# First stage of a hybrid encoder block: thirteen of 32 w_ada items multiplied by c on TensorE, small rows loaded through ScalarE's queue, gate transposes inside the second group

## The chip, the cores and the metric

One Trainium2 chip, of which the kernel uses one core. Time is the device time of one execution in microseconds (us). A core has TensorE (PE, matmuls; PEld its weight loads), VectorE (DVE), ScalarE (ACT), GpSimd (POOL) and SyncE (SP, which here only issues DMAs). Every engine runs its own instruction stream in order; semaphores tie them together.

## What is computed

One layer with a token mixer and an MLP, on x of 512 x 2048, each with RMSNorm and a shift, scale and gate that come from a conditioning vector c. The change lies in the part that these lines describe:

```python
c_act = jax.nn.silu(c)
mod = (c_act @ w_ada[i] + b_ada[i])[:, None, :]          # 2048 x 12288
shift_m, scale_m, gate_m, shift_f, scale_f, gate_f = jnp.split(mod, N_MOD, axis=-1)
h = rmsnorm(x, g_pre_mix[i]) * (1.0 + scale_m) + shift_m
proj = h @ w_in                                           # combined input projection
fq, fk, fv, ff, gq, gk, gv, ga, gr = jnp.split(proj, IN_OFFSETS, axis=-1)
log_f = jax.nn.log_sigmoid((ff + b_fgate).astype(jnp.float32))
```

What follows (forgetting attention on 8 heads, gated linear attention on 4, output projection, squared-ReLU MLP, residuals) is computed as before.

## The kernel before

All arithmetic is f32. A large product is made of three passes: each operand is split into a rounded part (`in_hi`, `w_hi`, written by ScalarE) and the rest (`in_lo`, `w_lo`, written by VectorE), and `split_mm` (L707 to L711) multiplies hi by hi, lo by hi and hi by lo.

The contraction over 2048 is cut into 16 steps k of 128 rows. The input projection runs in groups of six output tiles of 128 columns: group 0 (two heads of the forgetting attention), three more of these, then the GLA heads. One step of `group_steps` is 18 matmuls with 512 moving columns. Group 0 has besides three narrow ones each step (`wm_hi`, `wm_lo`: 16 gate-rank and 8 forget-gate columns), so 21. From group 1 on, small steps of the attention of the group before (`fox_slot`) are woven in between.

Group 0 can't use its input before scale and shift are there. Scale and shift for the mixer are 4096 columns of c_act @ w_ada. They are made in four blocks of 512 columns of either kind, and a block serves four steps k. A block is read as eight items (`load_am`, L537), each 256 rows of w_ada by 2 x 512 columns, 1 MB in two DMAs. Four buffers `am_item` hold items; item n is loaded when item n-4 has been used. `add_am` (L1662) on VectorE multiplies an item by its values of c, which are scalars of a partition, and adds to `am_acc`: two instructions of 128 x 1024. When all eight are in, TensorE sums over the 128 partitions with eight matmuls in which `am_acc` is stationary and one column of ones moves (`start_slot`, L901). `mod_columns_m` on VectorE adds the biases and gains (`mod_a`, `mod_b`), ScalarE writes `in_tmp` and `in_hi`, VectorE `in_lo`, and TensorE does the four steps. The items of the next block are multiplied meanwhile: VectorE's loop does two items after each step's `in_lo`.

Ahead of that, x comes in (`x_raw`), ScalarE squares it, POOL takes the root, VectorE scales it, TensorE transposes it in 64 pieces (L885) into six PSUM banks, and ScalarE and VectorE copy the banks to `xn_t`. Gains and biases arrive as rows (`rows_a`, `rows_b`, nine small DMAs by `as_rows`) on SP's queue behind the first four items, and are turned into columns (`cols_a`, `cols_b`); VectorE takes them between items 1 and 2 and scales x after item 3.

Between group 0 and group 1 the forget gate is made: VectorE and ScalarE compute log_sigmoid and a running sum (`f_z`), TensorE transposes it in four pieces (L937), ScalarE copies these to `cumq`, and TensorE waits for that copy before group 1. VectorE's order there is: gate operations, running sum, `w_lo` for group 1, eviction of its tiles of group 0.

Of the kernel before, what the change touches and what calls it, by code (L numbers as in the profile page):

```python
# [37 lines left out]
ALU = mybir.AluOpType  # L38
# [7 lines left out]
def build_block(nc, x, c, w_ada, b_ada, g_pre_mix, g_post_mix, w_in, b_fgate, w_gla_a2, b_gla_a2,  # L46
# [58 lines left out]
    with ExitStack() as ctx:  # L105
# [107 lines left out]
        decay = small("decay", [P, NCH])  # L213
        assert k_at[0] <= nc.sbuf_usable_end
# [64 lines left out]
        am_used = sem("am_used")  # L279
        am_sum = sem("am_sum")  # L280
# [91 lines left out]
        def arrived_mlp(b, mm):  # L372
            return RAW_MLP + 16 * (b * (MM_O // 2) + mm // 2 + 1)

# [80 lines left out]
        def _(sp):  # L455
# [79 lines left out]
            def as_rows(dst, src, done):  # L535
                sp.dma_start(dst, src.rearrange("o (k p) -> (o k) p", p=P)).then_inc(done, 16)

            def load_am(n):
                if n >= 4:
                    sp.wait_ge(am_used, n - 3)  # L540
# [9 lines left out]
            as_rows(rows_c[:, :], c[0:1, :], c_in)  # L550
# [6 lines left out]
            load_am(2)  # L557
            load_am(3)
            for n, src in enumerate((g_pre_mix[0:1, :], b_ada[0:1, SHIFT_M:SHIFT_M + D],
                                     b_ada[0:1, SCALE_M:SCALE_M + D], b_ada[0:1, SHIFT_F:SHIFT_F + D],  # L560
                                     b_ada[0:1, SCALE_F:SCALE_F + D], g_pre_mlp[0:1, :])):
                as_rows(rows_a[n * KT:(n + 1) * KT, :], src, rows_in)
            as_rows(rows_b[B_A2:B_GFOX, :], b_gla_a2, rows_in)
            sp.dma_start(rows_b[B_GFOX:B_GGLA, :], g_fox_out[0]).then_inc(rows_in, 16)
            sp.dma_start(rows_b[B_GGLA:20, :], g_gla_out[0].rearrange("h (k p) -> (h k) p", p=P)).then_inc(rows_in, 16)
            load_am(4)
            sp.wait_ge(wm_zero, 1)
            sp.dma_start(wm_raw[:, :, 0:RANK], w_in_t[:, :, GA_COL:GA_COL + RANK]).then_inc(wm_in, 16)
            sp.dma_start(wm_raw[:, :, 32:32 + FOX_HEADS], w_in_t[:, :, FF_COL:FF_COL + FOX_HEADS]).then_inc(wm_in, 16)
            sp.dma_start(b_fg[32:40, :], b_fgate.rearrange("o h -> h o")).then_inc(bfg_in, 16)  # L570
            load_am(5)
            load_fox(0, 0, wait=False)
            load_am(6)
            load_am(7)
# [131 lines left out]
        def _(pe):  # L706
# [6 lines left out]
            def group_steps(r, first, slot, misc_step=None):  # L713

                for k in range(KT):
# [10 lines left out]
                    for b in range(TILES):  # L726
# [10 lines left out]
                        if not first and b == 2:  # L737
                            slot(2 * k)
                    if not first:
                        slot(2 * k + 1)  # L740
# [13 lines left out]

            def fox_slot(s, f):

                if s == 0:
                    pe.wait_ge(ev_act, 3 * f + 3)
                    pe.wait_ge(ev_dve, 3 * f + 3)
                    for t in range(TB):  # L760
                        last = pe.transpose(BB[:, t * P:t * P + P], grp[:, VA, t * P:t * P + P], ident[:, :])
                    last.then_inc(fox_v_tr, 1)
# [5 lines left out]
                if s % 3 == 0 and s // 3 < 8:  # L768
                    j = s // 3
                    i = j % TB  # L770
                    if j:
                        pe.wait_ge(fox_max, 8 * f + j)
                    if j == 1:
                        pe.wait_ge(fox_v_tok, 2 * f + 2)
                    if j == 0:
                        pe.wait_ge(ada_col, 3 * f + Q_FOX)
                    q_tile, k_tile = (QA, KA) if j < TB else (QB, KB)
# [1377 lines left out]
```

## Time and profile before

| | us |
|---|---|
| median of three runs | 2357.48 (2356.92 to 2359.67) |
| profiled execution | 2364.44 |
| its span | 2362.4 |
| TensorE busy in the span | 2191.7 (93%) |
| VectorE busy | 1607.4 (68%) |
| ScalarE busy | 961.2 (41%) |
| group 0's matmuls, first to last | 62.67 to 177.33 |

All numbers of the sections below are from the profiled execution. Busy time of TensorE counts overlapping matmuls once. "Idle before" behind a row is the engine's idle time just before it, with what ended it. The granted clock (PEclk) is a share of 2.4 GHz: 0.50 is the lower level of 1.2 GHz. It is recorded where it changes; before the first change, at 54 us, the windows print 1.00.

### The profile page before, as it was taken

The page shows a single profiled execution, that of the slowest core. Times are in us where ns is not written, and L with a number is a line of the kernel's source. Part 1 is how long each engine was busy: PE and PEld are TensorE (multiplying, and loading weights), DVE is VectorE, ACT ScalarE, POOL GpSimd, SP SyncE. Part 2 cuts the span into 40 slices and gives each one's busy share as a digit, 9 for nine tenths or more (in the row PEclk, how much of TensorE's full clock was granted, in tenths as well). Part 3 has the DMA queues.
Part 4 walks back from the last instruction along what each step waited for, and adds up shares of the span by engine and source line. Part 5 has one row for each costly group of instructions (what it writes and reads, how often), then busy time and mean ns, then how long its engine had stood idle before and what let it go on. Part 6 is the DMA issues. An engine that isn't in the chain of part 4 may idle for free.

```text
span 2362.4 us, 26561 instructions
## 1 busy us (share of the span) xinstructions
PE 2191.7 (93%) x9759; PEld 1777.9 (75%) x9759; DVE 1607.4 (68%) x1418; ACT 961.2 (41%) x1445; POOL 489.3 (21%) x245
## 2 busy tenths in 40 slices
PE   2778999999999799989999999999989999999996
PEld 2566777777777577778888888888878888888875
DVE  5856666677787755466535436436469898998998
ACT  2225445444435423344434344344344444434443
POOL 0001221121111110110000000000026354544564
PEclk9889999999999999999999999999999999999998
DMA  8845545545555454256566666556346745766763
GB/s 310 302 166 148 160 135 149 154 132 156 156 159 162 128 200 130 71 183 209 214 209 196 219 200 211 212 191 227 134 143 214 246 161 187 243 214 208 273 207 150
DMA packets 335934, 441.09 MB, mean 187 GB/s; under 512 B 17036, under 2 KB 209744, under 8 KB 329816
## 3 DMA queue, kind: packets, MB, share of 16 engines
q1 hardware_dynamic: 335240, 435.51, 56.3%
q10 hardware_dynamic: 592, 4.21, 0.5%
q8 instruction: 66, 1.08, 0.2%
q14 instruction: 36, 0.29, 0.0%
HBM read 379.88 MB, written 59.79 MB: 186 GB/s over the span
## 4 chain that ended last, share of the span: by engine, by line
PE 56%; issue 31%; DVE 5%; POOL 5%; DVEq 1%; ACT 1%; POOLq 1%; DMA 0%; ACTq 0%
PE pair L709 18%; PE pair L711 18%; PE pair L710 18%; POOL ada L2030 3%; DVE acc L1506 1%; DVE v_op L1897 1%; POOL f_r L2063 1%; POOLq L2023 0%; POOL v_raw L2115 0%; PE pair L995 0%; POOL rstd L2024 0%; DVEq L1557 0%; ACT ada L1107 0%; DVE in_lo L1764 0%; DVE grp L1609 0%
## 5 line engine op out<-in xcount | busy, mean ns | idle before, releaser
L709 PE MATMUL pair<-in_hi,w_hi 128*128 128x512 f32 x1792 | 728.7, 407 | 10.9 <-DVE w_lo L1474 9.1
L711 PE MATMUL pair<-in_hi,w_lo 128*128 128x512 f32 x1792 | 705.7, 394 | 0.0
L710 PE MATMUL pair<-in_lo,w_hi 128*128 128x512 f32 x1792 | 705.5, 394 | 0.0
L1474 DVE TENSOR_TENSOR w_lo<-w_raw,w_hi 128x2048 fp32r<-128x2048 f32 (+1 forms) x142 | 301.2, 2121 | 379.1 <-ACT w_hi L1088 377.6
L1088 ACT ACTIVATE w_hi<-w_raw 128x2048 fp32r<-128x2048 f32 (+1 forms) x142 | 244.8, 1724 | 411.1 <-PE pair L711 337.4
L709 PEld LDWEIGHTS pair<-in_hi,w_hi 128*128 128x128 f32 x1792 | 341.4, 191 | 92.9 <-issue 20.9
L711 PEld LDWEIGHTS pair<-in_hi,w_lo 128*128 128x128 f32 x1792 | 340.5, 190 | 73.9
L710 PEld LDWEIGHTS pair<-in_lo,w_hi 128*128 128x128 f32 x1792 | 341.3, 190 | 70.1 <-issue 1.9
L709 PE MATMUL pair<-v_op,hid_r 128*128 128x512 f32 x896 | 349.9, 390 | 9.0 <-ACT v_op L1453 7.1
L711 PE MATMUL pair<-v_op,hid_r 128*128 128x512 f32 x896 | 349.3, 390 | 0.0
L710 PE MATMUL pair<-v_op,hid_r 128*128 128x512 f32 x896 | 349.3, 390 | 0.0
L1897 DVE TENSOR_TENSOR v_op<-v_raw,v_op 128x1024 fp32r<-128x1024 f32 x192 | 302.1, 1594 | 66.5 <-ACT v_op L1453 65.4
L1453 ACT ACTIVATE v_op<-v_raw 128x1024 fp32r<-128x1024 f32 x192 | 203.5, 1061 | 294.8 <-PE pair L711 280.2
L2030 POOL TENSOR_TENSOR ada<-ada,c_act 128x2048 f32<-128x2048 f32 x32 | 120.9, 3778 | 832.2 <-DMA ada<-in_w_ada 832.2
L1506 DVE TENSOR_REDUCE acc<-ada 128x128 f32<-128x2048 f32 x64 | 241.7, 3796 | 12.3 <-ACT ada L1107 12.0
L2106 POOL TENSOR_TENSOR v_sum<-v_raw,v_raw 128x512 f32<-128x512 f32 x64 | 157.1, 2482 | 350.5 <-DVE v_raw L1912 350.5
L709 PEld LDWEIGHTS pair<-v_op,hid_r 128*128 128x128 f32 x896 | 168.7, 188 | 45.8 <-ACT v_op L1453 7.5
L711 PEld LDWEIGHTS pair<-v_op,hid_r 128*128 128x128 f32 x896 | 168.6, 188 | 35.2
L710 PEld LDWEIGHTS pair<-v_op,hid_r 128*128 128x128 f32 x896 | 168.7, 188 | 35.1
L1107 ACT ACTIVATE ada<-ada,c_act 128x128 f32<-128x128 f32 x512 | 155.4, 388 | 6.4 <-DMA ada<-in_w_ada 6.4
L2115 POOL TENSOR_TENSOR v_raw<-v_raw,v_sum 128x512 f32<-128x512 f32 x64 | 143.3, 2269 | 18.5 <-DVE v_op L1897 18.4
L1928 DVE TENSOR_TENSOR y_t<-pair,y_t 128x1024 f32<-128x1024 f32 x104 | 125.0, 1215 | 0.9 <-PE pair L711 0.8
(194 smaller groups left out, 1908.1 us busy)
## 6 DMA issues: line engine op xcount, KB each, us to landing
ada<-in_w_ada SPq DMA_DIRECT2D x64, 1024.0 KB, 7.0
w_raw<-in_w_mlp_in SPq DMA_DIRECT2D x64, 1024.0 KB, 5.3
v_raw<-in_w_mlp_out SPq DMA_DIRECT2D x128, 512.0 KB, 4.9
hid_r<-hid_scratch SPq DMA_DIRECT2D x112, 512.0 KB, 6.3
hid_scratch<-hid_r SPq DMA_DIRECT2D x28, 1792.0 KB, 7.2
am_item<-in_w_ada SPq DMA_DIRECT2D x64, 512.0 KB, 5.2
w_raw<-in_w_in SPq DMA_DIRECT2D x128, 256.0 KB, 3.7
w_raw<-in_w_in SPq DMA_DIRECT2D x128, 128.0 KB, 3.5
```

The source lines that it names most:

```text
L709: pe.matmul(dst, a[0], b[0], start=start, stop=False, skip_group_check=onto)
L710: pe.matmul(dst, a[0], b[1], start=False, stop=False, skip_group_check=onto)
L711: return pe.matmul(dst, a[1], b[0], start=False, stop=stop, skip_group_check=onto)
L1088: act.activation(w_hi[n][:, view], w_raw[n][:, view], ACT.Copy).then_inc(hi_done, 1)
L1107: last = act.activation(ada0[0][:, k, :], ada0[0][:, k, :], ACT.Copy, scale=c_act[:, k:k + 1])
L1453: act.activation(v_op[i % 4][:, 0, :], raw_of(u, p)[:, h, :], ACT.Copy).then_inc(v_hi, 1)
L1474: dve.tensor_tensor(w_lo[n][:, view], w_raw[n][:, view], w_hi[n][:, view].bitcast(F32), ALU.subtract)\
L1506: dve.tensor_reduce(acc[:, u * P:(u + 1) * P], ada0[u][:, :, :].rearrange("p k n -> p n k"), AX_X, ALU.add).then_inc(ada_acc[u], 1)
L1897: dve.tensor_tensor(v_op[i % 4][:, 1, :], raw_of(u, p)[:, h, :], v_op[i % 4][:, 0, :].bitcast(F32), ALU.subtract).then_inc(v_lo, 1)
L2030: pool.tensor_tensor(unit[:, :, :], unit[:, :, :], c_act[:, :].rearrange("p (k o) -> p k o", o=1).to_broadcast([P, KT, P]), ALU.mult)\
L2106: last = pool.tensor_tensor(v_sum[:, h, cols], v_raw[q[B22]][:, h, cols], v_raw[q[B11]][:, h, cols], ALU.add)
L2115: last = pool.tensor_tensor(b21, b21, v_sum[:, h, cols], ALU.subtract)
```

## The change

- *Products of c on TensorE.* `AM_PE` names the items that TensorE takes: 1, 3, 5 and 7 of block 0, and 1, 3 and 5 of the other three blocks. `am_columns` does an item as 16 matmuls: a 128 x 128 piece of the item is stationary and one column of `c_act` moves; two row pieces are accumulated into one PSUM column. An item has eight columns of its own in bank 6. `mod_columns_m` adds the parts with one `tensor_reduce`, then goes on as before. VectorE keeps the other 19 items. An item that TensorE takes frees its buffer by `am_mul` instead of `am_used`.
- *Places.* Item 1 stands before the transposes of x, items 3, 5 and 7 behind them. Items 1, 3 and 5 of the next block stand before steps 1, 2 and 3 of the block at work. VectorE does items 0 | 2 | 4, 6 around the scaling of x and the eviction, and in a block items 0 | 2, 4 | 6, 7 after steps 1, 2 and 3.
- *Small rows.* The nine row loads go out first on ScalarE's queue; the two loads of narrow w_in columns and `b_fg` follow there behind the squares of x. SP's queue keeps c, x, the items and w_in.
- *Gate transposes.* The four transposes of `f_z` move from the gap between the groups into group 1, behind its third tile; the first logit moves behind its fifth tile, where TensorE waits for `cumq`. Group 1 is written out; the loop starts at group 2.

```diff
+        AM_PE = [(1, 3, 5, 7)] + [(1, 3, 5)] * 3
...
             def load_am(n):
                 if n >= 4:
-                    sp.wait_ge(am_used, n - 3)
+                    if on_pe(n - 4):
+                        sp.wait_ge(am_mul, items_before(n - 3, True))
+                    else:
+                        sp.wait_ge(am_used, items_before(n - 3, False))
...
+            def am_columns(n):
+                col = AM_COL + 8 * (1 + AM_PE[n // 8].index(n % 8))
+                pe.wait_ge(am_in[n % 4], 32 * (n // 4 + 1))
+                for part in range(2):
+                    for j in range(4):
+                        for kk in range(2):
+                            k = 2 * (n % 8) + kk
+                            last = pe.matmul(BA[:, col + 4 * part + j:col + 4 * part + j + 1],
+                                             am_item[n % 4][:, kk, part, j * P:j * P + P], c_act[:, k:k + 1],
+                                             start=kk == 0, stop=kk == 1)
+                last.then_inc(am_mul, 1)
+
+            am_columns(1)
             for k in range(KT):
                 if k == 0:
                     pe.wait_ge(xn_ready, TB)
+                    pe.wait_ge(cols_ready, 1)
...
+            for n in AM_PE[0][1:]:
+                am_columns(n)
...
             def start_slot(s):
...
+                if s % 8 and s // 8 < 3:
+                    if s % 8 == 2:
+                        pe.wait_ge(am_col, s // 8 + 1)
+                    am_columns(8 * (s // 8 + 1) + AM_PE[s // 8 + 1][s % 8 // 2 - 1])
                 if s % 8 == 0:
                     block = s // 8
-                    pe.wait_ge(am_used, 8 * (block + 1))
+                    pe.wait_ge(am_used, items_before(8 * (block + 1), False))
...
-            pe.wait_ge(cum_ready, 1)
-            for t in range(TB):
-                last = pe.transpose(BA[:, t * FOX_HEADS:(t + 1) * FOX_HEADS], f_z[32:40, t * P:t * P + P],
-                                    ident[32:40, 32:40])
-            last.then_inc(cumq_tr, 1)
-            pe.wait_ge(cumq_ready, 1)
-            with pe.Fori(1, FOX_GROUPS) as r:
+            group_steps(1, False, first_fox_slot, early=first_logit)
+            with pe.Fori(2, FOX_GROUPS) as r:
...
+            for n, src in enumerate((g_pre_mix[0:1, :], b_ada[0:1, SHIFT_M:SHIFT_M + D],
...
+                as_rows(rows_a[n * KT:(n + 1) * KT, :], src)
...
+            act.wait_ge(wm_zero, 1)
+            act.dma_start(wm_raw[:, :, 0:RANK], w_in_t[:, :, GA_COL:GA_COL + RANK]).then_inc(wm_in, 16)
+            act.dma_start(wm_raw[:, :, 32:32 + FOX_HEADS], w_in_t[:, :, FF_COL:FF_COL + FOX_HEADS]).then_inc(wm_in, 16)
...
-            for n in range(2):
-                add_am(n)
+            add_am(0)
...
-            for n in range(2, 4):
-                add_am(n)
...
-            for n in range(4, 6):
-                add_am(n)
+            add_am(2)
...
+                dve.wait_ge(am_mul, items_before(8 * (block + 1), True))
+                parts = BA[:, AM_COL:AM_COL + 8 * (1 + len(AM_PE[block]))].rearrange("p (s c) -> p c s", c=8)
+                dve.tensor_reduce(am_tot[:, :], parts, AX_X, ALU.add)
...
-            for n in range(6, 8):
+            for n in (4, 6):
                 add_am(n)
...
-                    for n in range(8 + 2 * k, 10 + 2 * k):
-                        add_am(n)
+                    for i in ((), (0,), (2, 4), (6, 7))[k % 4]:
+                        add_am(8 * (k // 4 + 1) + i)
```

TensorE from its first instruction to the first matmuls of group 0, before (a row's names are output, moving operand, stationary operand; `pair` is PSUM):

```order
L875 MATMUL pair<-ident,rows_c 128x16
L877 MATMUL pair<-ident,rows_a 128x96
L878 MATMUL pair<-ident,rows_b 128x20
L885 MATMUL pair<-ident,x_raw 128x128 x64
L901 MATMUL pair<-ones,am_acc_86 128x1 x8
L709 MATMUL pair<-in_hi,wm_hi 40x512
```

and the same place of the changed kernel, where L894 is a product of c and L927 the sum over the partitions:

```order
L881 MATMUL pair<-ident,rows_c 128x16
L883 MATMUL pair<-ident,rows_a 128x96
L884 MATMUL pair<-ident,rows_b 128x20
L894 MATMUL pair<-c_act,am_item_83 128x1 x16
L907 MATMUL pair<-ident,x_raw 128x128 x64
L894 MATMUL pair<-c_act,am_item_85 128x1 x16
L894 MATMUL pair<-c_act,am_item_83 128x1 x16
L894 MATMUL pair<-c_act,am_item_85 128x1 x16
L927 MATMUL pair<-ones,am_acc_86 128x1 x8
L708 MATMUL pair<-in_hi,wm_hi 40x512
```

Item 1 now stands ahead of the transposes, and items 3, 5 and 7 stand between them and the sum.

VectorE from the first column sums on, through one block of four steps, before:

```order
L1720 TENSOR_TENSOR mod_a<-mod_a,cols_a 128x4
L1726 TENSOR_TENSOR wm_lo<-wm_raw,wm_hi 128x640
L1707 TENSOR_TENSOR w_lo_78<-w_raw_74,w_hi_76 128x1536
L1702 TENSOR_TENSOR in_lo<-in_tmp,in_hi 128x512
L1676 TENSOR_SCALAR am_acc_87<-am_item_82,c_act 128x1024
L1674 SCALAR_TENSOR_TENSOR am_acc_87<-am_item_82,c_act,am_acc_87 128x1024
L1674 SCALAR_TENSOR_TENSOR am_acc_87<-am_item_83,c_act,am_acc_87 128x1024 x2
L1702 TENSOR_TENSOR in_lo<-in_tmp,in_hi 128x512
L1707 TENSOR_TENSOR w_lo_79<-w_raw_75,w_hi_77 128x1536
L1674 SCALAR_TENSOR_TENSOR am_acc_87<-am_item_84,c_act,am_acc_87 128x1024 x2
L1674 SCALAR_TENSOR_TENSOR am_acc_87<-am_item_85,c_act,am_acc_87 128x1024 x2
```

and changed:

```order
L1771 TENSOR_TENSOR mod_a<-mod_a,cols_a 128x4
L1777 TENSOR_TENSOR wm_lo<-wm_raw,wm_hi 128x640
L1754 TENSOR_TENSOR w_lo_78<-w_raw_74,w_hi_76 128x1536
L1749 TENSOR_TENSOR in_lo<-in_tmp,in_hi 128x512 x2
L1754 TENSOR_TENSOR w_lo_79<-w_raw_75,w_hi_77 128x1536
L1727 TENSOR_SCALAR am_acc_87<-am_item_82,c_act 128x1024
L1725 SCALAR_TENSOR_TENSOR am_acc_87<-am_item_82,c_act,am_acc_87 128x1024
L1749 TENSOR_TENSOR in_lo<-in_tmp,in_hi 128x512
L1725 SCALAR_TENSOR_TENSOR am_acc_87<-am_item_84,c_act,am_acc_87 128x1024 x2
L1725 SCALAR_TENSOR_TENSOR am_acc_87<-am_item_82,c_act,am_acc_87 128x1024 x2
```

The first two `in_lo` now come in a row, and one item instead of two pairs stands ahead of the third.

## Rows read from the trace of the kernel before

**Rows 1.** The page's slices of about 59 us, busy tenths of TensorE and VectorE.

```profile
PE   2778999999999799989999999999989999999996
DVE  5856666677787755466535436436469898998998
```

**Rows 2.** Windows, all engines: second and last block of group 0; columns in the heading.

```profile
core 0: us, PE busy (x) PEld busy (x) DVE busy (x) ACT busy (x) POOL busy (x), PEclk, DMA share, GB/s
93.67:124.74 31.07, 23.97 (x100) 18.07 (x101) 26.17 (x26) 8.32 (x11) 0.00 (x0) 0.88 0.92 322
156.16:177.33 21.17, 21.17 (x84) 15.98 (x84) 5.85 (x7) 6.32 (x8) 0.00 (x0) 0.91 0.13 37
```

**Rows 3.** Timeline of VectorE, third block; start us, duration, operation, [idle before].

```profile
129.27 0.69 DVE L1702 TENSOR_TENSOR in_lo<-in_tmp,in_hi 128x512 fp32r<-128x512 f32 x1
129.87 1.75 DVE L1474 TENSOR_TENSOR w_lo<-w_raw,w_hi 128x1536 fp32r<-128x1536 f32 x1
131.71 5.38 DVE L1674 SCALAR_TENSOR_TENSOR am_acc<-am_item,c_act,am_acc 128x1024 f32<-128x1024 f32 x4
...
152.95 0.16 DVE L1717 TENSOR_TENSOR mod_b<-pair,cols_a 128x4 f32<-128x4 f32 x1 [2.04 <-PE pair L901]
```

**Rows 4.** Timeline of TensorE, from the second block's end to the fourth's start.

```profile
117.34 0.39 PE L711 MATMUL pair<-in_hi,w_lo 128*128 128x512 f32 x1
119.91 1.95 PE L901 MATMUL pair<-ones,am_acc 128*128 128x1 f32 x16 [2.17 <-DVE am_acc L1674]
...
124.74 0.62 PE L709 MATMUL pair<-in_hi,wm_hi 128*40 128x512 f32 x1 [2.89 <-DVE in_lo L1702]
...
131.69 0.40 PE L709 MATMUL pair<-in_hi,wm_hi 128*40 128x512 f32 x1
...
156.16 0.62 PE L709 MATMUL pair<-in_hi,wm_hi 128*40 128x512 f32 x1 [3.25 <-DVE in_lo L1702]
```

**Rows 5.** Timeline, the first column sums.

```profile
55.40 3.54 PE L901 MATMUL pair<-ones,am_acc 128*128 128x1 f32 x16 [6.35 <-DVE am_acc L1674]
```

**Rows 6.** Windows of 1 us: PE busy, granted clock, DMA share, GB/s.

```profile
56.00:57.00 1.00, 1.00 (x6) 0.50 1.12 371
...
122.00:123.00 1.00, 0.00 (x0) 0.76 1.03 383
```

**Rows 7.** Timeline of all engines up to the first matmul of group 0.

```profile
6.76 0.75 DVE L1676 TENSOR_SCALAR am_acc<-am_item,c_act 128x1024 f32<-128x1024 f32 x1 [3.04 <-DMA am_item<-in_w_ada]
...
22.44 0.55 POOL L2024 TENSOR_TENSOR rstd<-ms,neg_half 128x1 f32<-128x1 f32 x1
...
33.90 4.87 DVE L1692 TENSOR_SCALAR x_raw<-x_raw,rstd 128x2048 f32<-128x2048 f32 x4
...
38.83 5.79 PE L885 MATMUL pair<-ident,x_raw 128*128 128x128 f32 x28 [11.02 <-DVE x_raw L1692]
...
44.90 4.15 PE L885 MATMUL pair<-ident,x_raw 128*128 128x128 f32 x36 [0.28 <-DVE xn_t L1698]
...
59.28 0.16 DVE L1720 TENSOR_TENSOR mod_a<-mod_a,cols_a 128x4 f32<-128x4 f32 x1
...
62.67 0.62 PE L709 MATMUL pair<-in_hi,wm_hi 128*40 128x512 f32 x1 [3.72 <-DVE w_lo L1707]
```

**Rows 8.** SP's queue: two issues, its longest wait, and the page's row of item loads.

```profile
18.86 0.37 SPq L536 DMA_DIRECT2D rows_b<-in_b_gla_a  x1
...
21.38 7.46 SPq L569 DMA_DIRECT2D wm_raw<-in_w_in  x1
...
SPq L544 <- DVE am_acc L1674: 68.1, 24, 8.3
...
am_item<-in_w_ada SPq DMA_DIRECT2D x64, 512.0 KB, 5.2
```

**Rows 9.** Timeline from the end of group 0 to the start of group 1.

```profile
176.94 0.39 PE L711 MATMUL pair<-in_hi,w_lo 128*128 128x512 f32 x1
...
180.13 1.76 DVE L1474 TENSOR_TENSOR w_lo<-w_raw,w_hi 128x1536 fp32r<-128x1536 f32 x1
...
182.14 0.79 PE L709 MATMUL pair<-in_hi,w_hi 128*128 128x512 f32 x1 [1.57 <-DVE w_lo L1474]
```

More of the change, by code:

```diff
@@ L213, in build_block @@
         decay = small("decay", [P, NCH])
+        am_tot = small("am_tot", [P, 8])
         assert k_at[0] <= nc.sbuf_usable_end
@@ L373, in arrived_mlp, with on_pe, items_before @@
             return RAW_MLP + 16 * (b * (MM_O // 2) + mm // 2 + 1)
+        AM_PE = [(1, 3, 5, 7)] + [(1, 3, 5)] * 3
+        def on_pe(n):
+            return n % 8 in AM_PE[n // 8]
+        def items_before(n, pe):
+            return sum(on_pe(i) == pe for i in range(n))
+        AM_COL = 192
         LAST = FBS - 1
@@ L556, in _ @@
             load_x(3)
[L557 to L571, printed above, removed]
+            for n in range(2, 5):
+                load_am(n)
             load_fox(0, 0, wait=False)
-            load_am(6)
-            load_am(7)
+            for n in range(5, 8):
+                load_am(n)
             load_fox(0, 1, wait=False)
@@ L738, in group_steps @@
                             slot(2 * k)
+                        if early and k == 0 and b == 4:
+                            early()
                     if not first:
@@ L753, in ada_rows, with fox_value, fox_logit @@
                 pe.matmul(dst[:, 0:2 * P], ones[:, :], acc[:, :], start=True, stop=True).then_inc(ada_sum, 1)
+            def fox_value(f):
+                pe.wait_ge(ev_act, 3 * f + 3)
+                pe.wait_ge(ev_dve, 3 * f + 3)
+                for t in range(TB):
+                    last = pe.transpose(BB[:, t * P:t * P + P], grp[:, VA, t * P:t * P + P], ident[:, :])
+                last.then_inc(fox_v_tr, 1)
+            def fox_logit(f, j):
+                i = j % TB
+                if j:
+                    pe.wait_ge(fox_max, 8 * f + j)
+                if j == 1:
+                    pe.wait_ge(fox_v_tok, 2 * f + 2)
+                if j == 0:
+                    pe.wait_ge(ada_col, 3 * f + Q_FOX)
+                q_tile, k_tile = (QA, KA) if j < TB else (QB, KB)
+                pe.matmul(BA[:, 0:(i + 1) * P], grp[:, q_tile, i * P:i * P + P], grp[:, k_tile, 0:(i + 1) * P],
+                          start=True, stop=True).then_inc(fox_qk, 1)
             def fox_slot(s, f):
                 if s == 0:
-                    pe.wait_ge(ev_act, 3 * f + 3)
-                    pe.wait_ge(ev_dve, 3 * f + 3)
-                    for t in range(TB):
-                        last = pe.transpose(BB[:, t * P:t * P + P], grp[:, VA, t * P:t * P + P], ident[:, :])
-                    last.then_inc(fox_v_tr, 1)
+                    fox_value(f)
                 if s == 1:
@@ L768, in fox_slot @@
                 if s % 3 == 0 and s // 3 < 8:
[L769 to L777, printed above, removed]
[L778 to L779 removed]
+                    fox_logit(f, s // 3)
                 if s % 3 == 2 and s // 3 < 8:
@@ L900, in start_slot @@
                         for j in range(4):
-                            last = pe.matmul(BA[:, 4 * part + j:4 * part + j + 1],
+                            last = pe.matmul(BA[:, AM_COL + 4 * part + j:AM_COL + 4 * part + j + 1],
                                              am_acc[block % 2][:, part, j * P:j * P + P], ones[:, 0:1],
```

49 lines of the change are left out of this document (33 added, 16 removed).

## The prediction

> **What bounds the kernel now.** I read the page's slices first: over most of the 2362 us TensorE is 90% busy or more, and only the first three slices (59 us each) are below that, where VectorE is the busier neighbour [rows 1]. The change touches only this first stage, so everything after its end is carried over unchanged, and the question is when group 1 of the input projection starts (before: 182.14 us).
>
> Second, the windows of the first group's blocks of four k-steps: in one block of 31.07 us TensorE is busy for 24.0 and VectorE for 26.2; in the last block, in which no w_ada item is left, 21.2 us of 21.2 are TensorE's [rows 2]. Third, VectorE's timeline in such a block: it multiplies items by c back to back (4 instructions, two items, in 5.38 us, so 2.69 an item and 21.5 for eight), with four in_lo of 0.69 and two w_lo of 1.75 between them [rows 3]; then it waits 2.04 us for the column sums. That is 27.8 us of work and some 3.5 of waits: VectorE sets the block, and SP waits 68.1 us in all for it to give item buffers back [rows 8]. Fourth, TensorE's timeline: the last 512-column matmul of a block starts at 117.34, the sums (L901) run 119.91 to 121.86, and the next block begins at 124.74; three blocks take from 62.67 to 156.16, 93.5 us [rows 4, 7]. TensorE's slack in a block is what waits between steps, about 5 us and no more.
>
> **The change part by part.**
>
> *The price of a product on TensorE.* The trace has no product of c there, but it has the same shape: L901, eight matmuls with a 128x128 f32 stationary tile and one moving column, leaves 16 records. At the upper clock 16 take 1.95 us, the last 0.25, so one starts every 0.113 us [rows 4]; at the lower clock 3.54, one every 0.213 [rows 5]. An item is 16 such matmuls, 32 records: 3.65 us, with the hand-over 3.75, at the upper clock, and 6.9 at the lower. VectorE paid 2.69 for it. So thirteen of the 32 items go from an engine that pays 2.69 to one that pays 3.75 to 6.9.
>
> *Start to the first matmul.* Nine issues of about 0.4 us [rows 8] now stand ahead of the exponential of c, which so ends near 5 instead of 3; item 0 lands only at 6.76 [rows 7], so 0. Today VectorE does items 0 to 3 and waits for the small rows before it scales x at 33.90, and the x transposes start at 38.83 [rows 7]. Now the rows go first on ScalarE's queue and only item 0 stands ahead of the scaling, so x is scaled as it comes: last square 22.0, POOL's root ends 23.0, scaling 1.3, transposes from 24.4 (item 1 on TensorE, 15 to 22 us, fits ahead of them). That is 14.4 us earlier. The transposes take 10.2 us [rows 7]. ScalarE evicts half of them and now issues the two w_in column loads just before; on SP the second issue stuck for 7.46 us [rows 8]. On ScalarE it may be stuck as long (to 31 us) or not at all; six banks cover TensorE until about 29.5, so I take 1 us, bounds 0 and 7. End 35.6. Then items 3, 5 and 7 on TensorE, in order. Item 7's load waits for item 3's product (39.3) and lands 5.2 later at the median [rows 8], 44.5, so it is ready when item 5 is done. No 512-column matmul is near, and the granted clock was 0.5 all through L901's 3.5 us at 56 us, and fell to 0.5 in 122 to 123, 5 us after the last 512-column matmul, although L901 had run in between [rows 4, 6]. I therefore take one item at the upper clock and two at the lower, 3.75 + 13.8 = 17.5: 53.1. From L901's start to mod_a takes 3.9 [rows 5, 7], the added reduce and drain 0.4, an estimate from the operations of 4 columns at 0.16 [rows 3]: 57.4. From mod_a to the first matmul 3.4, unchanged [rows 7]: 60.8. Before: 62.67. **-1.9 us.** The 14.4 us gained go to three products that stand in a row on TensorE.
>
> *The three blocks with items.* Steps 1, 2 and 3 of a block each have an item's product ahead of them. First step 6.95 (from 124.74 to 131.69, starting at the lower clock) [rows 4], three steps of 21 matmuls at 0.227, 14.3, three products 11.25: 32.5. Then L901 comes at once, VectorE being long done (five items 13.5 us, in all about 20), and from its start to the next block 4.83 [rows 4] and 0.4 for the reduce: 5.2. Block 37.7; the product takes up the 5 us of slack and pushes the rest. Three blocks 113.1 against 93.5: **+19.6 us.** Loads do not bind: sixteen transfers of 512 KB [rows 8] and two pieces of w_in are 10 MB a block, at today's 322 GB/s [rows 2] 31 us; item 15, whose buffer waits for item 11's product (about 19 us into the block), lands at 24 and is done by 27. What VectorE gives up is not late any more, so nothing of its 13 us comes back.
>
> *The last block* has no items: 21.2 us as today, 0.
>
> *Gate transposes into group 1.* TensorE's four small transposes leave the gap before group 1, but its first matmul waits for w_lo, which VectorE writes from 180.13 to 181.89, behind the scan of the gate, in the same order as now [rows 9]. So the gap from 177.33 to 182.14 stays: 0. In the group the first logit comes two tiles later, and VectorE and ScalarE's softmax chain has some slack in the step; bounds -1 and +2.
>
> Sum: -1.9 + 19.6 = **+17.7 us**. The profiled execution took 2364.4 us (span 2362.4); changed, 2382. The median of the runs is 7 us below that execution: 2357.5 + 17.7 = 2375.2, and I give 2375. Own range of this case 2365 to 2386 (the stuck issue +6, the clock falling inside two or three of the nine stretches of products +2 each; on the other side, one block start or two that stay at the upper clock, -2 each, and one product more at the upper clock ahead of the first block, -3).
>
> **Rivals.**
>
> *A. One-column matmuls keep the clock up.* Then all items ahead of block 0 cost 3.75: item 7 lands at 44.5, is done at 48.3, L901 takes 1.6 less, first matmul 54.4 (-8.3), and each of the four block starts saves the 2.1 us of its slow first step (6.95 against 4.8), -8.4. Sum -8.3 + 19.6 - 8.4 = +2.9: 2360, no change within 0.2%. Against: [rows 6], where L901 neither raised the clock nor held it; for: L901 is only 2 to 3.5 us long there with idle time on both sides, whereas a product stands between dense steps. Chance 0.17.
>
> *B. The clock falls in every stretch of products.* The stretch is 3.75 us without a 512-column matmul, and it fell about 5 us after one [rows 4, 6], so it should survive mostly. If not: nine times some 3.5 us at half speed, half of it lost and part of the product at 6.9: 2 to 3 each, +18 to +27, 2393 to 2402. Chance 0.08.
>
> *C. A product is cheaper than L901 tells (the other side).* Everything hangs on 0.113 us a record and two records a matmul. If one matmul of an item left one record, an item would cost 1.9 (3.5 at the lower clock). Item 3 ends at 37.5, item 7 lands at 42.7 and is done at 46.2 instead of 53.1, 6.9 less, and the blocks have 9 x 1.85 = 16.7 less. Sum 17.7 - 6.9 - 16.7 = -5.9: 2352, faster. It decides from about 2.0 us an item downwards for faster by more than 0.2%. For it speaks that the x transposes leave one record each; against it that even these, with 128 moving columns, start every 0.115 us [rows 7], so a pair of loads is what is paid, and L901 has the item's exact shape. Chance 0.08.
> The Trainium skill (TensorE: Matmul & The Clock Gate, Back-to-back issue gap) counts a matmul of up to 64 columns at about 60 cycles, by which a product would be under 1 us and this rival would win with some -17 us. By the same page (LDWEIGHTS) a load of 128 columns costs 107 ns in any case, and the trace's 0.113 agrees with that one.
> A rule of that page (Part 4: PE-mode transpose) says that transposes do not count as activity, by which item 3 would run at the lower clock too, another +3.1 (2378). The trace disagrees: 28 transposes took 5.79 us, the next 36 took 4.15 [rows 7].
>
> **How the numbers follow.** Likeliest case 0.67, A 0.17, B 0.08, C 0.08. About 0.2% (4.7 us) is what a measurement of this kernel can tell from no change. The best that order of work allows, with every stretch at the upper clock (A), is still +3, so faster needs C: 0.08, and 0.01 for what I have not seen. Same: A and 0.01 of the same kind, 0.18. Slower: the rest, 0.73. The range takes in A and the likeliest case to where the stuck issue and some falls of the clock add up: 2357 to 2390.
>
> **What would show it.** In the changed trace: x transposes starting near 24.5; 32 records of one column in 3.7 us between dense steps; the first in_hi matmul at 54 to 61; block starts 37 to 38 us apart (before 31); no wait of TensorE for in_lo inside a block; VectorE idle for a third of each block; group 1 starting near 200 and not 182, still behind w_lo. The forecast is wrong if products take under 3 us, if blocks come less than 34 us apart, or if group 1's first matmul no longer waits for w_lo.

## The result and the profile after

The changed kernel takes 2391.91 us (median of four, 2388.41 to 2394.88) against 2358.57 (four, 2356.92 to 2359.67) for the kernel before it on the same chip: 1.0139 times, 95% interval 1.0126 to 1.0151. Its profiled execution took 2394.88, the span 2393.1. The forecast was 2375, slower by 17.7; it is slower by 33.3, outside the range of 2357 to 2390. The direction was right, the size off by a factor of 1.9.

How much of that lies in the first stage can be read from one row, group 1's first matmul: 182.14 before [rows 9], 212.58 now, +30.44. The other 3 us are not in the traces: from group 1's first matmul to the end of the span takes 2180.3 us before and 2180.5 now. Over all profiled executions told of here the same part, with nearly the same instructions in it, takes 2168.7 to 2180.5. So below I compare kernels by the place of that matmul first and by their time second.

The changed kernel's timeline of TensorE up to group 0 (start us, duration, operation, [idle before]), which answers to [rows 5, 7]:

```profile
14.46 6.96 PE L894 MATMUL pair<-c_act,am_item 128*128 128x1 f32 x32 [3.36 <-DMA am_item<-in_w_ada]
23.73 5.38 PE L907 MATMUL pair<-ident,x_raw 128*128 128x128 f32 x24 [2.31 <-DVE x_raw L1740]
34.79 7.10 PE L907 MATMUL pair<-ident,x_raw 128*128 128x128 f32 x40 [5.68 <-ACT xn_t L1254]
41.72 9.02 PE L894 MATMUL pair<-c_act,am_item 128*128 128x1 f32 x64
50.91 6.99 PE L894 MATMUL pair<-c_act,am_item 128*128 128x1 f32 x32 [0.17 <-DMA am_item<-in_w_ada]
57.76 3.55 PE L927 MATMUL pair<-ones,am_acc 128*128 128x1 f32 x16
65.31 0.62 PE L708 MATMUL pair<-in_hi,wm_hi 128*40 128x512 f32 x1 [4.00 <-DVE w_lo L1754]
```

The transposes begin at 23.7 (forecast 24.4) and then stop for 5.68 us for ScalarE's eviction of `xn_t`. ScalarE and its queue at the same time:

```profile
19.43 0.41 ACTq L1249 DMA_DIRECT2D wm_raw<-in_w_in  x1
19.87 5.41 ACTq L1250 DMA_DIRECT2D wm_raw<-in_w_in  x1
21.19 0.19 ACT L1247 ACTIVATION_READ_ACCUMULATOR x_junk<-x_raw 128x1 f32 x1
25.31 8.79 ACTq L1251 DMA_DIRECT2D b_fg<-in_b_fgate  x1
34.14 1.57 ACT L1254 ACTIVATE xn_t<-pair 128x512 f32<-128x512 f32 x3 [12.76 <-issue]
```

The last two issues (the second `w_in` load and `b_fg`'s) take 14.2 us, and ScalarE evicts nothing for 12.76 us. In the kernel before, the second `w_in` load had stood 7.46 us on SP [rows 8], which computes nothing.

TensorE through the second block of group 0, cut to the products, the first matmul of each step and the sums; it answers to [rows 4]:

```profile
105.71 0.62 PE L708 MATMUL pair<-in_hi,wm_hi 128*40 128x512 f32 x1 [3.15 <-DVE in_lo L1749]
...
113.30 3.63 PE L894 MATMUL pair<-c_act,am_item 128*128 128x1 f32 x32
116.80 0.40 PE L708 MATMUL pair<-in_hi,wm_hi 128*40 128x512 f32 x1
...
121.59 3.62 PE L894 MATMUL pair<-c_act,am_item 128*128 128x1 f32 x32
125.08 0.45 PE L708 MATMUL pair<-in_hi,wm_hi 128*40 128x512 f32 x1
...
131.47 3.63 PE L894 MATMUL pair<-c_act,am_item 128*128 128x1 f32 x32
134.95 0.41 PE L708 MATMUL pair<-in_hi,wm_hi 128*40 128x512 f32 x1
...
141.35 1.84 PE L927 MATMUL pair<-ones,am_acc 128*128 128x1 f32 x16
...
146.34 0.62 PE L708 MATMUL pair<-in_hi,wm_hi 128*40 128x512 f32 x1 [3.15 <-DVE in_lo L1749]
```

The step behind the first product runs from 116.80 to the next product at 121.59, 4.8 us; the other two take 6.4 (125.08 to 131.47, 134.95 to 141.35) for the same 21 matmuls. Windows of the next block, around its first product (152.48 to 155.97), tell why (PE busy, granted clock, DMA share, GB/s):

```profile
155.00:156.00 1.00, 1.00 (x11) 1.00 1.07 414
156.00:157.00 1.00, 1.00 (x4) 0.52 0.44 168
157.00:158.00 1.00, 1.00 (x3) 0.50 0.75 100
158.00:159.00 1.00, 1.00 (x4) 0.50 0.90 320
159.00:160.00 1.00, 1.00 (x5) 0.78 1.03 396
160.00:161.00 1.00, 1.00 (x6) 1.00 1.06 394
```

The product itself runs at 2.4 GHz. As it ends the grant goes to 1.2 GHz, and the dense step behind it pays for some 3.5 us. In the three blocks seven of nine such steps are slow. The second block and the last block as windows (columns as in [rows 2], which they answer to):

```profile
105.71:146.34 40.63, 37.48 (x197) 31.54 (x197) 18.93 (x20) 8.30 (x11) 0.00 (x0) 0.84 0.72 247
187.17:207.92 20.75, 20.75 (x84) 15.63 (x84) 5.85 (x7) 6.33 (x8) 0.00 (x0) 0.93 0.15 39
```

TensorE is now 37.5 of 40.6 us busy where it was 24.0 of 31.1, VectorE 18.9 where it was 26.2. The gap between the groups, answering to [rows 9]:

```profile
207.53 0.39 PE L710 MATMUL pair<-in_hi,w_lo 128*128 128x512 f32 x1
...
210.72 1.76 DVE L1525 TENSOR_TENSOR w_lo<-w_raw,w_hi 128x1536 fp32r<-128x1536 f32 x1
...
212.58 0.77 PE L708 MATMUL pair<-in_hi,w_hi 128*128 128x512 f32 x1 [4.66 <-DVE w_lo L1525]
```

TensorE waits for `w_lo` as before.

### The profile page after: what moved, and what is told of

Read it like the earlier page. It is cut to its first block, busy times and chain, and to the rows that moved or that the text cites. A ratio compares the mean times of both kernels' runs of the same rounds, so it can differ in the third digit from the quotient of the medians.

```text
span 2393.1 us, 27332 instructions
## 1 busy us (share of the span) xinstructions
PE 2254.5 (94%) x10175; PEld 1840.4 (77%) x10175; DVE 1575.5 (66%) x1396; ACT 960.9 (40%) x1445; POOL 490.3 (20%) x245
## 4 chain that ended last, share of the span: by engine, by line
PE 57%; issue 29%; DVE 6%; POOL 4%; DVEq 2%; ACT 1%; DMA 1%; POOLq 0%; SPq 0%; ACTq 0%
PE pair L708 19%; PE pair L710 18%; PE pair L709 18%; POOL ada L2081 2%; DVE acc L1557 1%; DVE v_op L1948 1%; DVEq L1608 1%; DMA w_raw<-in_w_in 0%; POOLq L2074 0%; POOL v_raw L2166 0%; POOL rstd L2075 0%; PE pair L1031 0%; POOL f_r L2114 0%; DVEq L1594 0%; ACT ada L1143 0%
```

## The experiments

Eleven kernels. The edits are to the changed kernel unless another is named. Two theories stood at first: the cost comes from ScalarE's stuck issue and from the falls of the clock (theory 1), or simply from products that TensorE has no room for. The kernel before, run beside them, had medians of 2359.0 (first four), 2360.93 (next four) and 2360.86 (last three).

**1. Narrow loads back on SP's queue.**

```diff
 # sync
             for n in range(2, 5):
                 load_am(n)
+            sp.wait_ge(wm_zero, 1)
+            sp.dma_start(wm_raw[:, :, 0:RANK], w_in_t[:, :, GA_COL:GA_COL + RANK]).then_inc(wm_in, 16)
+            sp.dma_start(wm_raw[:, :, 32:32 + FOX_HEADS], w_in_t[:, :, FF_COL:FF_COL + FOX_HEADS]).then_inc(wm_in, 16)
+            sp.dma_start(b_fg[32:40, :], b_fgate.rearrange("o h -> h o")).then_inc(bfg_in, 16)
...
 # scalar
-            act.wait_ge(wm_zero, 1)
-            act.dma_start(wm_raw[:, :, 0:RANK], w_in_t[:, :, GA_COL:GA_COL + RANK]).then_inc(wm_in, 16)
...
```

> The changed kernel with one part undone: the two narrow w_in loads and b_fg are issued by SP again, behind item 4, as before; all else stays. In the changed trace ScalarE was held from 21.4 to 34.1 us by the issue of these loads and TensorE's transposes stood still for 5.7 us waiting for its copies. Theory 1 (the stuck issue is on the path): transposes run through from about 23.7 to 34.5, the first matmul of group 0 comes 6 to 7 us earlier (about 58.5 instead of 65.3), blocks unchanged at 40.4 to 40.8, so about 2385 where the changed kernel took 2391.9. Rival (the stall is hidden, the products behind the transposes wait for item loads anyway, or SP now gets stuck in its place and items 5 to 7 come later by as much): first matmul at 63 to 66, 2390 to 2392.

2387.24 us, 1.0124 [1.01, 1.0149]. Its timeline of TensorE, and SP's queue:

```profile
23.68 9.10 PE L911 MATMUL pair<-ident,x_raw 128*128 128x128 f32 x64 [2.31 <-DVE x_raw L1740]
32.62 3.63 PE L898 MATMUL pair<-c_act,am_item 128*128 128x1 f32 x32
37.15 13.21 PE L898 MATMUL pair<-c_act,am_item 128*128 128x1 f32 x64 [0.90 <-DMA am_item<-in_w_ada]
50.22 3.55 PE L931 MATMUL pair<-ones,am_acc 128*128 128x1 f32 x16
57.77 0.62 PE L712 MATMUL pair<-in_hi,wm_hi 128*40 128x512 f32 x1 [4.00 <-DVE w_lo L1754]
```

```profile
17.69 9.47 SPq L573 DMA_DIRECT2D wm_raw<-in_w_in  x1
```

The same load now holds SP, and TensorE waits 0.90 us for an item whose load stands behind it; but the transposes run without a stop and the first matmul of group 0 comes 7.54 us earlier. The blocks became 41.4, 41.1 and 41.05, since here the clock fell behind all nine products, so group 1 comes 5.70 earlier and the time is 4.7 lower. So the stuck issue on ScalarE is shown, at 7.5 us in the first matmul here; experiment 9 makes the same edit to the kernel of experiment 3, where it is worth 5.9 (64.95 to 59.01).

**2. The nine block products back on VectorE**, the four of block 0 left on TensorE.

```diff
-        AM_PE = [(1, 3, 5, 7)] + [(1, 3, 5)] * 3
+        AM_PE = [(1, 3, 5, 7), (), (), ()]
```

> The changed kernel with the nine products of blocks 1 to 3 given back to VectorE (two items after each step, as before); items 1, 3, 5, 7 of block 0 stay on TensorE. Theory (products in the blocks cost what the blocks got longer): block starts 31 us apart again instead of 40.4 to 40.8, first matmul at 65.3 as in the changed kernel, so 121.9 - 93.5 = 28.4 us less than 2391.9: 2363 to 2364, that is 5 us slower than before, 2.65 of it from the later first matmul. Rival (the loss is not in these products but in something that goes with them, as the loads behind PE's buffers or the added reduce): blocks stay above 34 us and the time above 2372.

2364.11 us, 1.0021 [1.0006, 1.0035]: 27.8 us lower. Blocks of 32.9, 31.9 and 32.9 and group 1 at 188.29, 24.3 earlier. So the blocks' products carry nearly all of the loss. The blocks are 0.8 to 1.9 us longer than in the kernel before. Here two of the three column sums ran at the lower clock and the third partly so (3.57, 3.58 and 2.56 us against 1.95 [rows 4]), which is 3.9 of the 4.2 us.

**3. The same nine products, spread.** The sixteen matmuls of a product stand in six portions behind the six tiles of their step, not in one stretch ahead of it. Nothing else changes: the same matmuls, the same items.

```diff
+            PIECES = ((0, 1), (1, 3), (3, 4), (4, 6), (6, 7), (7, 8))
+            def piece(k, b):
...
+                for q in range(*PIECES[b]):
+                    part, j = q // 4, q % 4
...
-                    am_columns(8 * (s // 8 + 1) + AM_PE[s // 8 + 1][s % 8 // 2 - 1])
```

> The changed kernel, but in the blocks each product of c is not one stretch ahead of a step: its 16 matmuls are spread over the six tiles of the same step, two or four behind each tile. The work, its operands and the items stay the same. In the changed trace seven of nine steps that followed a product took 6.4 us instead of 4.8, with the granted clock at 0.5 for about 3.4 us. Theory 1 (a 3.6 us stretch without 512-column matmuls lets the clock fall, and that is 11.4 of the 28 us that the blocks grew): no fall inside a block, steps with a product at 4.8 + 3.6 = 8.4, blocks about 36.8, time about 2380 to 2381. Rival (the clock falls with the share of one-column work however it is spread, or switching costs as much): 2388 or more.

2380.43 us, 1.0102 [1.0081, 1.0124]: 11.5 us lower than the changed kernel for an edit that only interleaves. Its first two blocks as windows:

```profile
64.95:102.00 37.05, 33.66 (x197) 28.67 (x198) 18.62 (x20) 7.48 (x10) 0.00 (x0) 0.91 0.60 201
102.00:139.20 37.20, 33.89 (x196) 28.80 (x197) 18.91 (x20) 8.41 (x11) 0.00 (x0) 0.91 0.79 268
```

The first matmul of each step with a product, first block:

```profile
71.48 0.40 PE L708 MATMUL pair<-in_hi,wm_hi 128*40 128x512 f32 x1
...
79.82 0.40 PE L708 MATMUL pair<-in_hi,wm_hi 128*40 128x512 f32 x1
...
88.17 0.40 PE L708 MATMUL pair<-in_hi,wm_hi 128*40 128x512 f32 x1
```

The clock of a block is 0.91 and not 0.84, and behind the first step, which starts at the lower clock as before, the grant stays at 1.00 up to the sums. A step with a product takes 8.35 us (4.8 and 3.55), and blocks take 37.05, 37.2 and 37.4, which is the 37.7 of the forecast within 0.7. Of the 28.4 us by which the three blocks had grown (121.9 against 93.5), then, 10.2 are the clock and 18.2 the products' own time beyond TensorE's slack.

**4. The gate transposes back in the gap.**

```diff
-            group_steps(1, False, first_fox_slot, early=first_logit)
-            with pe.Fori(2, FOX_GROUPS) as r:
+            pe.wait_ge(cum_ready, 1)
+            for t in range(TB):
+                last = pe.transpose(BA[:, t * FOX_HEADS:(t + 1) * FOX_HEADS], f_z[32:40, t * P:t * P + P],
+                                    ident[32:40, 32:40])
+            last.then_inc(cumq_tr, 1)
+            pe.wait_ge(cumq_ready, 1)
+            with pe.Fori(1, FOX_GROUPS) as r:
```

> The changed kernel with the gate transposes, cumq and the first logit put back between the groups, and the loop over groups from 1 again. Theory (moving them gained nothing, since group 1's first matmul waits for w_lo): 2391 to 2392, the same as the changed kernel, perhaps 0.3 to 1 us less. Rival (the move helped by some 2 to 4 us, as its place in the gap suggests): 2394 to 2396.

2392.83 us, 1.0154 [1.0134, 1.0175]. Group 1 starts at 213.39 with [1.39 <-DVE w_lo] before it. The first matmul (65.51) and the blocks (40.58, 40.79, 40.93) are the changed kernel's within 0.2 us each; here the clock fell behind eight of the nine products. Moving the transposes bought nothing and cost nothing that shows: `w_lo` decides either way.

**5. TensorE free at the start**: all eight items of block 0 on VectorE, narrow loads on SP, the blocks as in the change.

```diff
-        AM_PE = [(1, 3, 5, 7)] + [(1, 3, 5)] * 3
+        AM_PE = [(), (1, 3, 5), (1, 3, 5), (1, 3, 5)]
```

> The changed kernel with the narrow loads on SP (as the run before) and all eight items of block 0 on VectorE, items 1, 3, 5 of blocks 1 to 3 still on TensorE in one stretch each. Theory 1 (three products in a row on TensorE, two of them at the lower clock, are what ate the early transposes): VectorE does items 2 and 3 by 29 us and 4 to 7 from 34 to 45, so the first matmul of group 0 comes at 52 to 54 us instead of 57.8 of the run with the narrow loads on SP, blocks stay at 41: about 2382 to 2384. Rival (VectorE alone is no faster there, since its evictions and eight items add up to the same): first matmul at 57 to 60, 2387 or more.

2380.82 us, 1.0086 [1.0067, 1.0105]. The first matmul comes at 53.47, 9.2 us ahead of [rows 7] and 4.3 ahead of experiment 1: the early small rows and the early scaling of x are worth 9 us together, and the products on TensorE ahead of block 0 give almost half of it away. The blocks (41.5, 41.1, 41.2) take back more than that.

**6. One product a block**: item 3 alone, spread; block 0 as in the change; narrow loads on SP.

```diff
+        AM_PE = [(1, 3, 5, 7), (3,), (3,), (3,)]
```

> Narrow loads on SP; block 0 as in the changed kernel (items 1, 3, 5, 7 on TensorE); in blocks 1 to 3 only item 3 on TensorE, spread over the tiles of the block's second step. Theory (TensorE has 5 us of slack in a block of 31 and pays 3.6 a product, VectorE saves 2.7): blocks 30 to 30.8 us, first matmul at 57.8, so 5 plus 1 to 3 us less than before: 2351 to 2354. Rival (any product on TensorE costs its full price): blocks at 33 to 35, 2360 or more.

2353.62 us, 0.9971 [0.9959, 0.9982], faster than before. Blocks of 29.5, 30.1 and 30.4 against 31.0 to 31.4 [rows 2, 4, 7]: one product fits into TensorE's slack, and VectorE, down to seven items, is ready in time (TensorE waits for `am_acc` in no block, where it had waited 2.17 us [rows 4]). The first matmul is at 58.84.

**7. No product on TensorE**, x still scaled early, narrow loads on SP, gate transposes back.

```diff
+        AM_PE = [(), (), (), ()]
```

> Only the order of the start is changed against before: small rows first on ScalarE's queue, x scaled as it comes, all 32 items on VectorE, narrow loads on SP, gate transposes between the groups. Theory (the early rows are worth the whole gain, without any product on TensorE): first matmul at 52 to 54 us instead of 62.67, blocks 31.1 as before, 8 to 10 us less than before: 2349 to 2351. Rival (VectorE has the same sum of work up to the first block, so what is scaled early is paid back): first matmul at 60 or later, 2357 or more.

2347.3 us, 0.9946 [0.9929, 0.9963]. First matmul 53.37, blocks 31.55, 32.4, 31.7, group 1 at 174.89. The products have no part in this gain, so in the first stage it is the early small rows and the early scaling of x, which no experiment takes apart. The first stage explains 7.25 us of it (group 1 against [rows 9]); the time fell by 13.6, and where the other 6 us come from stays open.

**8. Both**: as 7, with items 1 and 5 of block 0 and item 3 of the other blocks on TensorE, the latter spread.

```diff
+        AM_PE = [(1, 5), (3,), (3,), (3,)]
```

> As the last one, with items 1 and 5 of block 0 and item 3 of the other blocks on TensorE (item 1 ahead of the transposes, item 5 behind them beside VectorE's 4, 6 and 7, item 3 spread over the tiles of a step). Theory: first matmul at 50 to 51.5 us, blocks 30 to 30.8, so 2 us at the start and 1 to 3 in the blocks less than that kernel: 2344 to 2348. Rival (the loads or the single column sums bind already, or the clock falls more): the same as that kernel within 1 us, or slower.

2342.35 us, 0.9919 [0.99, 0.9939], the fastest of all. Blocks 29.08, 29.87 and 30.25, group 1 at 169.89, 12.25 before [rows 9]; the time fell by 18.6, so 6 us of it are not explained by the first stage. The first matmul missed its 50 to 51.5:

```profile
23.91 10.22 PE L916 MATMUL pair<-ident,x_raw 128*128 128x128 f32 x64 [2.33 <-DVE x_raw L1768]
37.97 6.99 PE L903 MATMUL pair<-c_act,am_item 128*128 128x1 f32 x32 [3.83 <-DMA am_item<-in_w_ada]
46.26 3.55 PE L935 MATMUL pair<-ones,am_acc 128*128 128x1 f32 x16 [1.31 <-DVE am_acc L1753]
53.80 0.62 PE L715 MATMUL pair<-in_hi,wm_hi 128*40 128x512 f32 x1 [3.99 <-DVE w_lo L1783]
```

Item 5 came 3.83 us too late, and its product then ran at the lower clock. The first matmul is 0.4 us later than in experiment 7, so what this kernel gains over that one is in the blocks (89.2 against 95.6), not at the start.

**9. Both cures on the changed kernel**: experiments 1 and 3 together.

> The changed kernel with both cures at once: the two loads of narrow w_in columns and b_fg on SP's queue, and every block product spread behind the six tiles of its step. Theory (the stuck issue on ScalarE and the falls of the clock are two separate costs and add up): first matmul of group 0 near 57.8, blocks near 37.2, group 1 near 195.5 (17 later than in the changed kernel), time near 2374. Rival (they overlap, as the first cure alone gave back a third of its gain in the blocks): blocks over 38.5 and group 1 later than 199.

2372.57 us, 1.0062 [1.0041, 1.0082]. First matmul 59.01, blocks 38.22, 37.22 and 37.68, group 1 at 198.55: 14.0 earlier than in the changed kernel, where 1 and 3 alone gave 5.7 and 9.7. The two costs add within 1.4 us; group 1 is 3 us later than I wrote and only 0.5 short of the rival's border. What is left at group 1 is 16.4 us: 19.6 in the blocks, which is the forecast's own term, -3.7 at the first matmul and +0.4 behind the blocks.

**10. Experiment 8 with the block's product in one stretch.**

```diff
-                        if first:
-                            piece(k, b)
...
+                    am_columns(8 * (s // 8 + 1) + AM_PE[s // 8 + 1][s % 8 // 2 - 1])
```

> The best kernel so far (items 1 and 5 of the first block and item 3 of the other three on TensorE) with the one product of a block in one stretch ahead of its step instead of spread. Theory (each stretch lets the clock fall and costs 1.6 us where TensorE sets the pace): the step after it takes 6.4 and not 4.8, block starts up to 1.6 later each, 3 to 5 us on the time, near 2346. Rival (with one product a block TensorE has slack enough and VectorE's seven items set the block): the step is slower but the blocks stay at 29 to 30.3, time within 1 us of the spread one.

2349.56 us, 0.9952 [0.9936, 0.9969]; experiment 8 had 2342.35. Blocks 30.38, 30.52 and 30.68, 2.4 us more in all, and group 1 at 171.73, 1.84 later. Behind the product the step took 4.8, 6.4 and 6.4 us: two falls of three, 3.2 us, less what the first steps of the blocks happened to differ. The theory's slow step is there behind two products of three, and the blocks are longer, so the rival is out; but 2.4 us in the blocks is less than the theory's 3 to 5, and the 7.2 between the two times are more. Some 5 us of these lie behind group 1's start and are not explained by the stretch.

**11. Experiment 8 with the narrow loads late on ScalarE's queue.**

```diff
             act.wait_ge(xt_dve, KT // 2)
+            act.wait_ge(wm_zero, 1)
+            act.dma_start(wm_raw[:, :, 0:RANK], w_in_t[:, :, GA_COL:GA_COL + RANK]).then_inc(wm_in, 16)
...
+            first_hi(0)
             act.wait_ge(wm_in, 32)
             act.activation(wm_hi[:, :, :], wm_raw[:, :, :], ACT.Copy).then_inc(wm_hid, 1)
-            first_hi(0)
```

> The best kernel so far with the two loads of narrow w_in columns and b_fg on ScalarE's queue behind its last eviction of xn_t, where ScalarE then has nothing to do for 13 us. Theory (the many-piece load holds whichever queue issues it; on SP it delayed items 5 to 7): SP is not held, item 5 is there when TensorE is free at 34, its product is done near 38, first matmul of group 0 near 50 to 51 instead of 53.8, time 2 to 3 us lower, near 2340. Rival (the items' transfers, not their issue, bind the start): item 5's product still waits to 37 or later and the first matmul stays at 53 or later.

2350.39 us, 0.9959 [0.9946, 0.9972]: slower than experiment 8, not faster. TensorE, then ScalarE:

```profile
34.01 3.63 PE L899 MATMUL pair<-c_act,am_item 128*128 128x1 f32 x32
43.25 3.54 PE L931 MATMUL pair<-ones,am_acc 128*128 128x1 f32 x16 [5.62 <-DVE am_acc L1753]
58.35 0.62 PE L711 MATMUL pair<-in_hi,wm_hi 128*40 128x512 f32 x1 [11.55 <-DVE in_lo L1778]
```

```profile
35.42 4.71 ACTq L1283 DMA_DIRECT2D wm_raw<-in_w_in  x1
40.16 9.51 ACTq L1284 DMA_DIRECT2D b_fg<-in_b_fgate  x1
49.71 1.48 ACT L1288 ACTIVATE w_hi<-w_raw 128x1536 fp32r<-128x1536 f32 x1 [15.35 <-issue]
54.27 0.74 ACT L1299 ACTIVATE wm_hi<-wm_raw 128x640 fp32r<-128x640 f32 x1 [3.07 <-DMA wm_raw<-in_w_in]
```

Half of each theory is true. With SP free the items do come in time: item 5's product follows the transposes at once and at the upper clock, and the sums start 3.0 us earlier (43.25 against 46.26). So it was the issue on SP that had held the items in experiment 8. But ScalarE is held for 14.2 us here too, and the load landed at 54.2, so that `wm_hi` and all behind it came late. I had counted the time that ScalarE has nothing to do (13 us), not what the load needs.

All together (us; blocks are the three with items):

| | first matmul | three blocks | group 1 | time | ratio |
|---|---|---|---|---|---|
| before | 62.67 | 93.5 | 182.14 | 2358.6 to 2360.9 | |
| changed | 65.31 | 121.9 | 212.58 | 2391.91 | 1.0139 |
| 1 narrow on SP | 57.77 | 123.6 | 206.88 | 2387.24 | 1.0124 |
| 2 blocks VectorE | 64.96 | 97.7 | 188.29 | 2364.11 | 1.0021 |
| 3 spread | 64.95 | 111.7 | 202.84 | 2380.43 | 1.0102 |
| 4 gate back | 65.51 | 122.3 | 213.39 | 2392.83 | 1.0154 |
| 5 start VectorE | 53.47 | 123.7 | 202.70 | 2380.82 | 1.0086 |
| 6 one a block | 58.84 | 90.0 | 175.63 | 2353.62 | 0.9971 |
| 7 none on TensorE | 53.37 | 95.6 | 174.89 | 2347.30 | 0.9946 |
| 8 both | 53.80 | 89.2 | 169.89 | 2342.35 | 0.9919 |
| 9 spread, on SP | 59.01 | 113.1 | 198.55 | 2372.57 | 1.0062 |
| 10 one stretch | 54.59 | 91.6 | 171.73 | 2349.56 | 0.9952 |
| 11 narrow late | 58.35 | 90.0 | 175.26 | 2350.39 | 0.9959 |

## Why the prediction was wrong

**The step that failed most: the blocks' term, by leaving out the clock.** It put three blocks at 113.1 us; they took 121.9, 8.8 more. Seven slow steps of nine at 1.6 us each are 11.3 more, and products of 3.5 instead of 3.75 give 2.2 back; the last 0.3 back are in the first steps and the sums. The forecast named the mechanism as rival B and gave it 0.08, on the ground that in [rows 4, 6] the grant fell 5 us after the last 512-column matmul, so that a stretch of 3.75 us should survive. That used one sighting as a bound. The one-column matmuls are the same kind of work as L901, of which the same rows say that they do not hold the clock; the right reading was that any of the nine may fall, and rows before could not say how many. B's price for each (2 to 3 us) was too high, since the product itself keeps the upper clock; 1.6 was paid. Its time, 2393 to 2402, is nearest to the 2391.91 measured. Experiment 3 shows the mechanism alone: with the stretches broken up the blocks take 37.05 to 37.4, 111.7 in all.

**The second: 1 us for ScalarE's stuck issue, bounds 0 and 7.** From their start to their end the transposes took 18.0 us (23.73 to 41.72) where the forecast had 11.2, so the issue's price was 7.8, above even the upper bound. TensorE's cover was right (it stopped at 29.1; I had 29.5). What was wrong is how long ScalarE is held: I put the end at 31, with the 7.46 us of [rows 8] for one issue, and counted nothing for `b_fg`'s load behind it, because it is tiny. It is just this one that stood 8.79 us, to 34.1. And a stop costs more than itself: the other 40 transposes began at the lower clock and took 7.10 us, where 40 at 0.115 [rows 7] would be 4.6. Experiment 1 prices the whole at 7.5 us in the first matmul, experiments 3 and 9 at 5.9. The forecast of the first matmul missed by 4.5 (65.31 against 60.8): + 6.8 for the issue, - 0.7 since the transposes began early, - 1.5 since the three products took 16.0 and not 17.5, and - 0.1 behind the sums.

The Trainium skill (DMA: Bandwidth & Descriptors, Issuing engines are not separate DMA queues) says that a second issuing engine saves only the sequencer's time, "which is usually small relative to the DMA itself". Here the three issues took 14.6 us of the 19.2 from the first issue to the landing of the last piece (34.98 to 54.2, experiment 11), so for loads cut into 4096 short pieces the measurement does not agree.

**The sum.** +17.7, + 8.8 in the blocks, + 4.5 at the start, - 0.6 from the last block on, is + 30.4, which is group 1's shift. The profiled executions (2364.44 and 2394.88) differ by the same 30.4. The other 3 us of the + 33.3 stand between the medians alone: the one before lies 5.9 below its profiled execution, the one after 3.0. I leave them open; they are within what the rest of the kernel varies by between executions, and experiment 4 shows no gain or loss from the gate transposes.

**What held.** The price of a product on TensorE (3.63 us of records, 3.5 to the next step, against 3.75; 6.96 to 6.99 at the lower clock, against 6.9), read from L901's records, so rival C, by which the change would have been faster, is out. By the figure in the Trainium skill (TensorE: Matmul & The Clock Gate, Back-to-back issue gap) for matmuls of up to 64 columns it would have been under 1 us, an estimate from that figure; the trace disagrees. The same section of the Trainium skill says that the gap of an isolated matmul is too low at few columns because it leaves out the weight loads, and here each matmul has a stationary tile of its own. The price of a record is not the same at either clock: 0.113 us at the upper, 0.213 at the lower [rows 4, 5]. Further: TensorE sets the blocks, and VectorE's relief is worth nothing there; the loads do not bind in them; `w_lo` alone starts group 1; the gate transposes are worth 0 (experiment 4); the transposes of x start at 23.7, which I put at 24.4; the first column sums to the first matmul, 7.55 for 7.7. Rival A is out: the products held the clock up in no better than two of nine places. Two readings were wrong without harm: in [rows 1] the fourth slice of TensorE is below 90% too, and in the third VectorE is not the busier one; and VectorE idle for a third of a block did not fit the forecast's own 20 us of work in 37.7 (it was busy for 18.9 of 40.6).

## What to carry to other kernels

Work that is moved to an engine with little slack is paid in full beyond the slack: one product a block of 3.5 us made this kernel faster, three made it slower. On TensorE count besides it the dense work that runs at the lower clock behind any stretch of one-column matmuls, and spread such a stretch among wide ones, which cost under 0.1 us a product (8.35 against 3.5 and 4.8) and saved 10 us here. Before a DMA is moved to a computing engine's queue, take the longest duration that its issue shows in the trace as time in which that engine computes nothing, count the DMAs behind it too, and ask what waits for that engine meanwhile; a change with several parts is best taken apart, since here the harmful part hid a good one (experiment 7: group 1 starts 7.25 us earlier, and the time is 13.6 lower).

## What the runs showed of the hardware

- A product of sixteen one-column f32 matmuls that stands alone between dense steps takes 3.63 us, all at the upper clock, and the grant goes to 0.50 as it ends or up to 1.4 us later. It did so behind 7 of 9 in the changed kernel, 8 of 9 in experiment 4, 9 of 9 in experiments 1 and 5, and 2 of 3 in experiment 10, and not once where the sixteen were spread among wide matmuls (experiments 3, 6, 8, 9 and 11). Which of them escape is not settled. Of a block's first products, the three that escaped came after a first step of 7.52 to 7.59 us, and all the others after 6.1 to 7.30; but one that escaped in the changed kernel was the second of its block.
- 128-column f32 transposes raise the clock and hold it: in the changed kernel the grant was 0.50 from 34 to 39 us and 1.00 from 40 on, and TensorE did only these transposes from 34.8 to 41.7. The product right behind them ran at 1.00, and the grant fell at 46.9, in the second one. In experiment 1 the 64 took 9.10 us and the product right behind them 3.63; where 3.83 us of idle time came between (experiment 8), the product took 6.99.
- Of the two loads of 2048 short pieces each (64 and 32 bytes) the first is issued in 0.4 us, the second holds whichever sequencer issues it: SP for 7.46 us in the kernel before and for 9.46 to 9.48 in the experiments, ScalarE for 5.41 (changed kernel) and 4.71 (experiment 11). The next DMA, `b_fg`'s of 8 elements, stood another 8.79 and 9.51 on ScalarE's queue and 1.00 to 1.93 on SP's. The sums are 8.5 us on SP before, 10.6 to 11.4 on SP in the experiments and 14.2 on ScalarE. Why the queues divide it so differently is not settled.
